# Attention projection: value units stored in two groups of tiles, cached parts stored between kinds of unit; attention's loop over head pairs written out

## The reference

```python
q, k, v, g = jnp.split(h @ w_in, 4, axis=-1)        # attn_project
...
qs = apply_rope(qs, cos, sin)
ks_ = apply_rope(ks_, cos, sin)
k_all = jnp.concatenate([ks_, k_ctx], axis=1)       # k_ctx, cache_v: cached keys and values
v_all = jnp.concatenate([vs, cache_v[:, j]], axis=1)
...
s = jnp.einsum('bqhcd,bkhcd->cbhqk', qi, k).astype(jnp.float32) * scale
p = jax.nn.softmax(s, axis=-1)
a = (p[0] - lam * p[1]).astype(v.dtype)
return jnp.einsum('bhqk,bkhv->bqhv', a, v)
...
o = rms_norm(o, subln) * (1.0 - lam_init)
return gated_out(o.reshape(b, n, D_INNER), g, w_out)
```

## Time and profile before

| | |
|---|---|
| median of three runs | 2510.16 us |
| the profiled execution | 2514.49 us |
| its span | 2512.7 us |
| PE busy | 2261.2 us (90%) |
| DVE / ACT / POOL busy | 1132.8 / 775.8 / 163.8 us |
| mean granted TensorE clock | 0.943 of 2.4 GHz |
| DMA traffic | 353.49 MB, mean 141 GB/s |

### The profile page before, as it was taken

The page is one execution under the profiler, slowest core; times in us unless marked ns, Lnnn a source line. Parts: engine busy times, 40 slices in busy tenths (PEclk is TensorE's granted clock), DMA queues, the critical chain, the costliest instruction groups (busy, mean ns, idle before and its releaser), DMA issues. The chain is left out here.

```text
span 2512.7 us, 34709 instructions
## 1 busy us (share of the span) xinstructions
PE 2261.2 (90%) x13793; PEld 2160.9 (86%) x13793; DVE 1132.8 (45%) x1559; ACT 775.8 (31%) x1321; POOL 163.8 (7%) x68
## 2 busy tenths in 40 slices
PE   6799879969996999999798899969989899997996
PEld 1799857969995999999798899969888788887995
DVE  2745195363115444444311211117767677774112
ACT  2421043123113111111111112116656566664111
POOL 0200000000012121212000000000000000000100
PEclk9899799889997999999899999989999999998997
DMA  6544244275224545464533322152444433207224
GB/s 277 204 166 164 77 170 150 88 290 199 79 73 173 175 123 151 123 154 127 135 126 123 124 102 97 64 201 110 159 160 159 160 111 121 90 19 264 76 94 169
DMA packets 125360, 353.49 MB, mean 141 GB/s; under 512 B 12368, under 2 KB 63696, under 8 KB 117072
## 3 DMA queue, kind: packets, MB, share of 16 engines
q1 hardware_dynamic: 124112, 347.41, 40.4%
q10 hardware_dynamic: 1152, 4.72, 0.5%
HBM read 237.23 MB, written 114.82 MB: 140 GB/s over the span
## 5 line engine op out<-in xcount | busy, mean ns | idle before, releaser
L434 PE MATMUL p_ps<-p_h_hi,p_w_hi 128*128 128x384 f32 x1536 | 353.7, 338 | 37.5 <-DVE p_h_lo L527 32.8
L434 PE MATMUL p_ps<-p_h_lo,p_w_hi 128*128 128x384 f32 x1536 | 352.4, 337 | 0.0
L434 PE MATMUL p_ps<-p_h_hi,p_w_lo 128*128 128x384 f32 x1536 | 351.7, 337 | 0.0
L434 PEld LDWEIGHTS p_ps<-p_h_hi,p_w_hi 128*128 128x128 f32 x1536 | 276.9, 190 | 41.1 <-issue 28.4
L434 PEld LDWEIGHTS p_ps<-p_h_lo,p_w_hi 128*128 128x128 f32 x1536 | 277.0, 190 | 0.0
L434 PEld LDWEIGHTS p_ps<-p_h_hi,p_w_lo 128*128 128x128 f32 x1536 | 276.6, 190 | 0.0
L1280 PE MATMUL o_ps<-o_y_hi,o_w_hi 128*128 128x384 f32 x768 | 177.1, 338 | 35.3 <-DVE o_w_lo L1334 32.6
L421 PE MATMUL p_ps<-p_w_hi,p_h_hi 128*128 128x256 f32 x576 | 169.0, 293 | 34.2 <-DVE p_cut_lo L584 34.2
L1703 DVE TENSOR_REDUCE a_nmax<-a_ps 128x1 f32<-128x1152 f32 (+1 forms) x143 | 176.2, 1232 | 23.7 <-PE a_ps L1551 21.1
L1637 ACT ACTIVATE a_e<-a_ps,a_nmax 128x1152 f32<-128x1152 f32 (+1 forms) x143 | 161.3, 1128 | 72.3 <-DVE a_nmax L1703 72.3
L1588 PE MATMUL a_ps<-a_v_hi,a_at_hi 128*128 128x256 f32 x584 | 177.8, 304 | 6.4 <-DVE a_g L1758 4.9
(11 more groups left out here) (223 smaller groups left out, 3828.9 us busy)
## 6 DMA issues: line engine op xcount, KB each, us to landing
p_w_raw<-w_in_dram SPq DMA_DIRECT2D x40, 1024.0 KB, 6.1
g_dram<-p_stage SPq DMA_DIRECT2D x32, 576.0 KB, 3.0
f_w_raw<-w_u_dram SPq DMA_DIRECT2D x32, 512.0 KB, 3.8
o_w_raw<-w_out_dram SPq DMA_DIRECT2D x32, 512.0 KB, 4.3
f_g<-g_dram SPq DMA_DIRECT2D x8, 1152.0 KB, 7.8
y_dram<-f_y SPq DMA_DIRECT2D x8, 1152.0 KB, 5.3
x_dram<-o_x_new SPq DMA_DIRECT2D x16, 576.0 KB, 5.0
q_hi_dram<-p_cut_hi SPq DMA_DIRECT2D x32, 288.0 KB, 4.3
```

The source lines that it names most:

```text
L434: mm = pe.matmul(ps[:, 4 * b + c, 0:CH], a, x[:, c * CH:(c + 1) * CH], start=(d == 0 and j == 0), stop=(d == DT - 1 and j == 2))
```

## The change

1. A value unit's stores go out in two groups. When tiles 0 to 3 are drained, SP stores v_hi's four tiles and v_lo's in two pieces, counted on `stored[0]`; after tile 8 it stores tiles 4 to 8 of both and new_v in one piece, counted on `stored[1]`. ACT waits for `stored[0]` before tile 0 and for `stored[1]` before tile 4. So there are six stores a unit, with three counted on each semaphore.
2. Before the first unit only the cached keys are loaded and split. `loops` calls `after(kind)` between kinds: behind the q units SP issues the stores of the cached keys and the load of the cached values, and ACT and DVE split these there; behind the k units SP issues their stores.
3. `rotations` in `attention` writes out all four pairs; PE, ACT and DVE have no loop there any more.

```diff
-"value": 2}[what]
+"value": 3}[what]
...
+            for kind, k in enumerate(plan):
+                if kind > 0 and after is not None:
+                    after(kind - 1)
...
+        VA = 4
...
-                for c, kept in enumerate(("k", "v")):
-                    if c == 1:
-                        sp.wait_ge(past_lo_done, 1)
-                    sp.dma_start(past_raw[:, :], past[kept]).then_inc(past_in, 16)
-                    sp.wait_ge(past_lo_done, c + 1)
-                    for x, part in ((past_hi, "hi"), (past_lo, "lo")):
-                        sp.dma_start(out[f"{kept}_past_{part}"], x[:, :].bitcast(F32)).then_inc(past_out, 16)
+                sp.dma_start(past_raw[:, :], past["k"]).then_inc(past_in, 16)
+
+            def after(kind):
+
+                if rope is None or kind > 1:
+                    return
+                sp.wait_ge(past_lo_done, kind + 1)
+                for x, part in ((past_hi, "hi"), (past_lo, "lo")):
+                    sp.dma_start(out[f"{'kv'[kind]}_past_{part}"], x[:, :].bitcast(F32)).then_inc(past_out, 16)
+                if kind == 0:
+                    sp.dma_start(past_raw[:, :], past["v"]).then_inc(past_in, 16)
...
                     if k["what"] == "value":
+                        v_out = [out[part][n].rearrange("(t p) v -> p t v", p=P) for part in ("v_hi", "v_lo")]
+                        sp.wait_ge(drained[p], k["drain"][p] + i * TT + VA)
+                        sp.dma_start(v_out[0][:, 0:VA], v_hi[:, 0:VA].bitcast(F32)).then_inc(stored[0], 16)
+                        sp.dma_start(v_out[1][:, 0:2], v_lo[:, 0:2].bitcast(F32)).then_inc(stored[0], 16)
+                        sp.dma_start(v_out[1][:, 2:VA], v_lo[:, 2:VA].bitcast(F32)).then_inc(stored[0], 16)
                         sp.wait_ge(drained[p], k["drain"][p] + (i + 1) * TT)
-                        for x, part in ((v_hi, "v_hi"), (v_lo, "v_lo")):
-                            sp.dma_start(out[part][n].rearrange("(t p) v -> p t v", p=P), x.bitcast(F32)).then_inc(stored[0], 16)
-                        for c in range(2):
-                            cols = slice(c * P, (c + 1) * P)
-                            sp.dma_start(out["new_v"][n][:, cols], v_new[:, cols]).then_inc(stored[1], 16)
+                        for x, into in ((v_hi, v_out[0]), (v_lo, v_out[1])):
+                            sp.dma_start(into[:, VA:TT], x[:, VA:TT].bitcast(F32)).then_inc(stored[1], 16)
+                        sp.dma_start(out["new_v"][n], v_new[:, :]).then_inc(stored[1], 16)
...
+            def after(kind):
+                if rope is not None and kind == 0:
+                    past_split(1)
...
-                        for b in range(2):
-                            act.wait_ge(stored[b], k["stored"][b] + 16 * k["stores"] * n)
                         for t in range(TT):
+                            if t in (0, VA):
+                                act.wait_ge(stored[t // VA], k["stored"][t // VA] + 16 * k["stores"] * n)
...
-            for m in range(2):
-                rotate(0, m, False)
-            with eng.Fori(0, H // 2 - 1) as i:
-                for m in range(2, STEPS + 2):
-                    rotate(i, m, False)
-            for m in range(2, STEPS + 2):
-                rotate(H // 2 - 1, m, True)
+            for pair in range(H // 2):
+                last = pair == H // 2 - 1
+                for m in range(0 if pair == 0 else 2, STEPS + 2):
+                    rotate(pair, m, last)
```

More of the change, by code:

```diff
@@ L301, in project @@
         for n, (what, name, units) in enumerate(kinds):
-            stores = {"plain": 1, "silu": 1, "rope": 6 if name == "k" else 4, "value": 2}[what]
+            stores = {"plain": 1, "silu": 1, "rope": 6 if name == "k" else 4, "value": 3}[what]
             per = TT if what == "value" else 2
@@ L312, in project, with loops @@
                 stored0[s] += 16 * stores * units
-        def loops(eng, body):
-            for k in plan:
+        def loops(eng, body, after=None):
+            for kind, k in enumerate(plan):
+                if kind > 0 and after is not None:
+                    after(kind - 1)
                 if k["last"]:
@@ L397, in body @@
                                 sp.dma_start(out["new_k"][n, c, b], stage[rows, b, NS:T]).then_inc(stored[b], 16)
-            loops(sp, body)
+            loops(sp, body, after)
             for b in range(2):
@@ L475, in _, with past_split @@
                 op.then_inc(h_hi_done, 1)
-            if rope is not None:
[L477 to L481, removed]
+            def past_split(c):
+                act.wait_ge(past_in, 16 * c + 16)
+                if c == 1:
+                    act.wait_ge(past_out, 32)
+                act.copy(past_hi[:, :], past_raw[:, :]).then_inc(past_hi_done, 1)
+            def after(kind):
+                if rope is not None and kind == 0:
+                    past_split(1)
+            if rope is not None:
+                past_split(0)
             def body(k, i, last):
@@ L508, in body @@
                         act.activation(split3(stage[:, b, :]), banks(b), func).then_inc(drained[b], 1)
-            loops(act, body)
+            loops(act, body, after)
         @block.vector
@@ L529, in low_half, with past_split, after @@
                 op.then_inc(h_lo_done, 1)
+            def past_split(c):
+                dve.wait_ge(past_hi_done, c + 1)
+                if c == 1:
+                    dve.wait_ge(past_out, 32)
+                dve.tensor_tensor(past_lo[:, :], past_raw[:, :], past_hi[:, :].bitcast(F32),
+                                  ALU.subtract).then_inc(past_lo_done, 1)
+            def after(kind):
+                if rope is not None and kind == 0:
+                    past_split(1)
             inverse_rms.vector(dve)
@@ L600, in body @@
                                           ALU.subtract).then_inc(cut_lo_done, 1)
-            loops(dve, body)
+            loops(dve, body, after)
             if w_ada is not None:
```

## The result

| | before | after | |
|---|---|---|---|
| median of four runs | 2510.97 us | 2471.74 us | ratio 0.9846, 95% interval 0.9834 to 0.9858 |
| the profiled execution | 2514.49 us | 2470.78 us | |
| its span | 2512.7 us | 2469.0 us | -43.7 us |
| PE busy | 2261.2 us | 2245.1 us | |
| mean granted clock | 0.943 | 0.950 | |

The kernel is 39.2 us faster, where 45 were forecast; 2471.7 us lies in the range 2459 to 2476 and 6.3 us above the forecast.

The account below looks back on a forecast made before the run. PE was taken to bound the kernel, so its gaps count: -29.75 - 5.7 - 6.4 + 15.2 - 18.1 = -44.75 us, from the median 2510.16 us to 2465.4 us. Range 2459 to 2476 us.

Parts of the forecast that it names:

- second q unit's gap: Projection's start: PE's 4.68 us wait at the second q unit and its 1.7 us slow restart go; 6.4 us gained.
- second k unit's stall: Between q and k units: the cached values' chain stalls PE 13.5 us, plus 1.7 us slow restart; 15.2 us lost.
- first value unit: Its tile 0 waits only for the last k unit's b = 0 stores; gain 5.7 us, bounds 3 and 6.5.
- seven boundaries: Between value units: seven gaps with their slow restarts, 4.25 us each, go; 29.75 us gained.
- attention: Attention written out: the loop's two issue gaps and their slow restarts go, 9.4 + 8.7 = 18.1 us gained.
- rival (a): Stall between q and k larger (8 us) or value unit's tile 4 waits (10 us): 2474 to 2484 us; chance 0.12.
- Rival (b): Attention: the gaps are not the jump's but come back elsewhere, so writing out gives nothing: 2483.5 us; chance 0.05.
- Rival (c): Attention: written-out code stalls where its blocks are fetched, 9.05 us each, slower than before from the fifth on; chance 0.02.
- 9.7 + 1.7 = 11.4: Between q and k: the trio's 9.73 us at the stage's start, plus 1.5 to 2 us for the q stores' remainder.
- one price for every restart: PE's slow restart at 1.2 GHz, taken at 1.7 us from the 4.68 us gap at the second q unit.
- some 23 us: Upper bound of the q-to-k stall: remainder, 3 MB and weights' 1 MB all at 209 GB/s instead of 321.
- the 1.4 us a unit: Value units: loss if the second group or queue were late by its full old measure; gain at least 20 us.

Follow-up runs that it names:

- early load: The change, but SP stores cached keys and loads cached values before the q units, with the split left between q and k units: 2452.99 us, 0.9774 to before.
- value units alone: Before with only the value units' stores in two groups, cached parts and attention's loop as before: 2476.18 us, ratio 0.9872.
- both moves: The change with cached values loaded before the q units and the value units' halves in xs, stores counted apart: 2448.2 us, ratio 0.9752 to before.
- value halves in xs: The change with the value units' high and low halves in tile xs, their stores on own semaphores: 2463.79 us, ratio 0.9814 to before.
- without the cached parts' move: The change with the cached parts handled at the start as before: 2460.36 us, ratio 0.9804 to before.
- cached parts alone: Before with only the cached keys' stores and cached values' split moved between q and k units: 2520.75 us, ratio 1.0044.
- all waits before tile 0: The change, but ACT waits for both groups of stores before tile 0: 2476.61 us, ratio 0.9872 to before.
- attention alone: Before with only attention's loop over head pairs written out: 2493.71 us, ratio 0.9933.
- the last kernel: Early cached-value load, value halves in xs, and value units' ACT and DVE splitting next weights behind tile 3, against the change: 2446.44 us, ratio 0.9748 to before.

## Why the prediction was right, and where it was off

From the two traces, place by place (the slow restart counted with its gap):

| term of the sum | predicted, us | measured, us | from |
|---|---|---|---|
| second q unit's gap | -6.4 | -6.4 |; no wait there after |
| second k unit's stall | +15.2 | +17.0 | 14.38 us gap, 2.65 us restart |
| first value unit | -5.7 | -5.0 | from its start to its tile 8: 42.7 us, now 37.7 |
| seven boundaries | -29.75 | -29.75 | 211.19 us, now 181.44 |
| attention | -18.1 | -18.1 | 503.4 us, now 485.3 |
| sum | -44.75 | -42.25 | |

The spans differ by 43.7 us; 0.9 of the rest arose ahead of the projection's first unit, which the change doesn't touch.

Each mechanism was the one that the prediction named, and no rival came in; the stall between q and k went rival (a)'s way, but by 1.8 us and not by 8. Rival (a)'s wait before tile 4 never happened: new_v lands 7.2 us after tile 8, with 7.2 us to spare before tile 4. Rival (b), gaps that come back elsewhere: none in attention. Rival (c), fetches that stall in the written-out code: none in seven stretches.

Three sizes were off, two of them in the step on the second k unit. The trio of transfers (two stores and the load of the cached parts) took 1031.06 - 1018.83 = 12.23 us from its first issue instead of 9.7 + 1.7 = 11.4. The 2.5 us above the 9.7 are not all the remainder of the q stores, as the prediction had it: the DMA engines moved 364 GB/s meanwhile, 4.48 MB, which is the trio's 3.15, some 0.57 left of the q stores and some 0.76 of the weight load issued at 1022.47. The kernel after:

```profile
1018.80:1031.10 12.30, 6.88 (x40) 6.56 (x38) 0.00 (x0) 0.04 (x1) 0.00 (x0) 0.90 0.98 364
```

The second is the restart there. It was taken at 1.7 us, from the 4.68 us gap; behind the 14.38 us gap it is 2.65: seven groups of three matmuls take 1046.36 - 1040.07 = 6.29 us where they need 3.64. The third is the first value unit, which gave 5.0 us and not 5.7. Its gap shrank as forecast, from 15.14 us to 9.42, but the slow phase behind it grew from 2.9 us to 4.6. The kernel before, then the kernel after, each from PE's start until the full rate is back:

```profile
1231.70:1234.60 2.90, 2.90 (x13) 2.90 (x14) 0.69 (x2) 0.04 (x1) 0.00 (x0) 0.51 0.49 206
```

```profile
1235.70:1240.30 4.60, 4.60 (x22) 4.60 (x23) 0.67 (x2) 0.01 (x1) 0.00 (x0) 0.51 0.99 238
```

So the failing step is one price for every restart, read at one gap. The trace of before already spoke against it: PE's timeline, first unit of the projection, behind a gap of only 3.27 us:

```profile
805.26 1.33 PE L434 MATMUL p_ps<-p_h_hi,p_w_hi 128*128 128x384 f32 x3 [3.27 <-DVE p_h_lo L527]
...
811.78 0.68 PE L434 MATMUL p_ps<-p_h_lo,p_w_hi 128*128 128x384 f32 x3
```

Seven groups take 6.52 us here, so 2.9 us are lost, more than behind 4.68 us or behind 15.14.

Two bounds of the prediction don't follow from its rows. The "some 23 us" for the stall is the time in which 4.78 MB move at 209 GB/s; as a loss it would be 22.9 + 9.02 - 6.9 + 1.7 = 26.7 us, so by that term rival (a) reached to 2477. And the 1.4 us a unit in the lower bound of part 1 has no working behind it.

The prediction took the chain of the cached values as one piece that moves, and it didn't ask which link of it makes the loss. The early load answers that: the split fits where the change puts it, and only its data came late.

Of the 6.3 us between forecast and median, the terms explain 2.5 (44.75 against 42.25), and the median of before, which another run moved up to 2510.97, explains 0.8. The rest is no term: the traces' terms come to 42.25 us and the timed runs to 39.2, 3.0 us less, with an interval of some 3 us to either side. The parts alone give 33.9 + 16.3 - 10.7 = 39.5 us, so they agree with the whole. The prediction took its terms from an execution 4.3 us above the median and set the sum against the median, as if all terms held alike in every execution. Some of them don't: what the restart behind the 14 us stall costs is 1.9, 2.0, 2.7 and 2.9 us in the four profiled kernels that have it. Whether the missing 3 us are that, or chance in the runs, isn't settled.

The two pages of the Trainium skill that were held against each other can now be judged in this kernel. Its "Runtime: NRT & Kernel Launch", section "Instruction fetch mechanics", says that a jump to code outside the fetched window stalls; the run with PE alone written out agrees, with 19 us for two jumps. The 108 ns of the Trainium skill's "Advanced Engine Details and Errata", section "Control Flow Timing", can't be the whole price of such a jump. The projection's own loops jump back too, and none of their edges shows an idle time on PE, with no block fetched in 140 us of the k units; what body size separates the two was not tried.

## What to carry to other kernels

When a step is moved to where its engines have time, move only the engines' part: what it needs from memory should be asked for well ahead, here where it was. Asked for only when it is needed, the load comes late by its own time and by that of all that is issued before it, and holds everything that is queued after it. A unit that waits for all of its predecessor's stores is cured by making the last group of stores small and early enough, before any wait is moved. An idle time of the bound engine that is put down to nothing, at the edge of a long loop, is worth writing out on that one engine; the trace of the code behind the loop's exit tells beforehand what it will bring, and the DMA view of the gap whether instructions are fetched in it. The price of a restart should be read at several gaps and given as a range, not as one number.

## What the runs showed of the hardware

After most gaps PE runs at 1.2 GHz for some time, and what that costs doesn't go by the gap's length. The granted clock right after two gaps, first the kernel before, then the kernel after:

```profile
831.70:834.70 3.00, 3.00 (x10) 3.00 (x11) 2.47 (x2) 0.00 (x0) 0.35 (x1) 0.52 1.01 306
```

```profile
1040.10:1045.80 5.70, 5.70 (x18) 5.70 (x19) 2.44 (x2) 0.41 (x1) 3.09 (x2) 0.51 0.00 0
```

PE was at 1.2 GHz for about 3 us after 4.68 us idle, and for 5.7 us after 14.38 us idle. By these two alone a longer gap would cost more, but the 15.14 us gap above had only 2.9 us of slow phase, and the 3.27 us gap 5.9. At that last place, with the same gap, the kernel with the early load lost next to nothing (PE's timeline):

```profile
804.62 0.79 PE L447 MATMUL p_ps<-p_h_hi,p_w_hi 128*128 128x384 f32 x3 [3.29 <-DVE p_h_lo L547]
...
808.39 0.68 PE L447 MATMUL p_ps<-p_h_lo,p_w_hi 128*128 128x384 f32 x3
```

Seven groups take 3.77 us where they need 3.64. The time lost in the restart (what the matmuls take above 0.52 us for a group of three, or 0.12 us for one of a value unit's), from the traces of several kernels:

| gap, us | lost, us |
|---|---|
| 3.3 | 0.1 (early load), 1.4 (value units alone), 2.9 (before) |
| 5.2 | 1.8 (both moves), 2.5 (value halves in xs) |
| 9.4 | 1.6 (early load), 2.1 (the change), 2.4 (without the cached parts' move), 2.6 (value units alone) |
| 14.1 to 14.6 | 1.9 (cached parts alone), 2.0 (all waits before tile 0), 2.7 (the change), 2.9 (value halves in xs) |
| 15.1 to 15.3 | 1.3 (before), 1.6 (attention alone), 2.1 (cached parts alone), 2.2 (all waits before tile 0) |

So at one place, with one gap, the cost differs by 0.7 to 2.8 us from execution to execution. What sets it these runs don't show.

Even the 2.49 us gap of the last kernel isn't free. PE's timeline of it, single matmuls:

```profile
1211.06 0.39 PE L437 MATMUL p_ps<-p_w_hi,p_h_hi 128*128 128x256 f32 x1 [2.49 <-DVE p_xs L617]
1211.28 0.28 PE L437 MATMUL p_ps<-p_w_lo,p_h_hi 128*128 128x256 f32 x1
...
1212.36 0.40 PE L437 MATMUL p_ps<-p_w_lo,p_h_hi 128*128 128x256 f32 x1
...
1215.76 0.29 PE L437 MATMUL p_ps<-p_w_hi,p_h_lo 128*128 128x256 f32 x1
```

PE restarts at the full rate and falls to the slow one only 1.3 us later, for 3.4 us: 16 matmuls in 3.40 us, where 0.12 us each make 1.92. So the slow phase can come after the work has begun again, and here it costs 1.5 us for a gap of 2.5. The seven boundaries of the kernel before, 4.25 us each, are made of the same: gaps of 2.5 to 2.8 us, and some 1.6 us lost to a slow phase behind six of them and none behind the seventh.
